# Column blocks of 384, 352 and 352 tokens in place of 368, 368 and 352 in two projections of a streaming encoder layer

## The chip, the cores and the metric

The kernel runs on one core of one Trainium2 chip. The metric is the device time of one execution in microseconds (us), from runs of the whole kernel; the profile comes from one further execution, the profiled one, whose own time is given beside its span.

## What is computed

One layer of a hybrid encoder runs over 1024 prompt frames with 16 meta tokens ahead of them, and over 64 frames of a running stream. All is fp32.

```python
hn = rmsnorm(h, norm_mix_w)
proj = hn @ w_in                      # 1024 -> 3584: xt, b, c, q, k, v, g
conv_out = b * conv3(c * xt)          # causal, depthwise, 512 channels
o = retention(rotary(q), rotary(k), v)   # 4 heads of 128, per-head decay
ret_out = silu(g) * groupnorm(o) * ret_gn_w
h = h + concat([conv_out, ret_out]) @ w_out
f = square(relu(rmsnorm(h, norm_ffn_w) @ w_up)) @ w_down   # 1024 -> 4096 -> 1024
y = rmsnorm(h + f, norm_final_w)
```

The outputs are y for both streams, the last two conv inputs and the retention states.

## The kernel before

Every large product is made of fp32r matmuls on a value split in two parts, hi and lo: `passes` (L1510) issues three matmuls, hi by hi (L1512), hi by lo (L1513) and lo by hi (L1514), and each of them has a weight load of its own, 128x128, before it. In the two projections that the change is about, the activations stand transposed in SBUF, with the 1024 model channels as eight k-tiles of 128 partitions and the tokens as columns; a 128x128 piece of the weight matrix is the stationary operand, and up to 512 token columns stream past it into a PSUM bank.

The work runs in this order:

- Start: the input is normalised, transposed tile by tile into `hn_hi` and `hn_lo`, and `v` is computed.
- In-projection, `iteration` (L1651), four times, one per head and group of 128 channels: six units k, q, g, xt, c, b. A unit is 128 output channels for all tokens. It is done in two halves of four k-tiles (the weight buffers `ws_hi`, `ws_lo` hold one half each), and each half goes over three column blocks of tokens. The lists `CGX` (k, 1104 tokens with the meta tokens), `CGQ` (q, g, b, 1088 tokens) and `CGC` (xt, c, 1090 tokens) give each block's first column and width. A block in a half is 4 k-tiles by 3 passes, so 12 matmuls. A block has a PSUM bank of its own, and the units take two sets of three banks in turn (`set_of`). `bank_free` (L1580) is the wait for the bank. Between blocks the table `AFTER` puts the steps of the retention, `step`, on TensorE.
- Out-projection over nine token tiles, with the second norm and the transposes into `mid_hi` and `mid_lo`.
- FFN, 16 groups of 256 hidden channels. `up` (L1734) computes two units of 128 hidden channels, again in halves of four k-tiles over three column blocks, given by `CGY`. ScalarE takes each block with `relu` (L815) and squares it. Then `product` makes 28 products of 128x128 by 128x512 (the down projection, with seven products in place of eight for each 2x2 block) and `sample` four more for the 64 frames of the running stream. VectorE, ScalarE and GpSimd add them to `h`. The 28 products and the sample are 92 matmuls of 512 columns. The last group ends in plain products and the final norm.

Who takes the blocks of the in-projection: VectorE turns k and q in `rotary` (L1058, four operations for a block, with `rot` of `BLK` columns as scratch) and multiplies c and b; ScalarE takes g and xt. The order of the work on each engine is written out by hand, and no planner decides anything.

Where the column blocks begin and end in SBUF follows from these lines (`TX` is 1104, `TY` 1088, `TP` 1152; the tensors' first bytes are multiples of 128):

```python
        hn_hi = sb("hn_hi", [P, KT, TX], r1, F32R)
        hn_lo = sb("hn_lo", [P, KT, TX], r1 + KT * TX * 4, F32R)
        mid_hi = sb("mid_hi", [P, KT, TP], r2, F32R)
        mid_lo = sb("mid_lo", [P, KT, TY], r2 + KT * TP * 4, F32R)
        rot = sb("rot", [P, BLK], region(BLK * 4))
```

Of the kernel before, what the change touches and what calls it, by code (L numbers as in the profile page):

```python
# [51 lines left out]
TP = TY + SAMPLE  # L52
TILES = (TY + P - 1) // P
XTILES = (TX + P - 1) // P
BLK = 368
CGX = [(0, 368), (368, 368), (736, 368)]
CGQ = [(0, 368), (368, 368), (736, 352)]
CGC = [(0, 368), (368, 368), (736, 354)]
META_AT = [META - 2, META - 1, *range(META - 2)]
CGY = [(0, 368), (368, 368), (736, 352)]  # L60

CONV = [(0, SEQ, META - 2), (SEQ, SAMPLE, META + SEQ)]

UNITS = [("k", 3 * DC + DC, CGX), ("q", 3 * DC, CGQ), ("g", 3 * DC + 3 * DC, CGQ),
         ("xt", 0, CGC), ("c", 2 * DC, CGC), ("b", DC, CGQ)]
V_OFF = 3 * DC + 2 * DC
# [68 lines left out]
def build(nc, x_prompt, x_sample, state_conv, state_ret, meta_tokens, norm_mix_w, w_in, conv_w, ret_gn_w,  # L135
# [3 lines left out]
    with ctx:  # L139
# [4 lines left out]
        def region(size):  # L144
            at = place["at"]
            place["at"] = at + (size + 31) // 32 * 32
            return at

        def sb(name, shape, at, dt=F32):
            return nc.alloc_sbuf_tensor_at(name, shape, dt, offset=at)  # L150
# [71 lines left out]
        onC = sb("onC", [P, HD], region(512))  # L222
        rot = sb("rot", [P, BLK], region(BLK * 4))
        hc = sb("hc", [P, NCONST], region(NCONST * 4))
# [368 lines left out]
        def _(act):  # L593
# [127 lines left out]
            def conv_hi(i, j):  # L721
                act.wait_ge(proj_dve, NX + i * 12 + 9 + j + 1)
                col, n = CGQ[j]
                act.activation(mid_hi[:, bass.ds(i, 1), col:col + n].rearrange("p a c -> p (a c)"),
# [90 lines left out]
            def relu(g, a, j):  # L815
                col, w = CGY[j]
                act.wait_ge(up_done, 6 * g + 3 * a + UP_ORDER[a].index(j) + 1)
                act.activation(fr[:, a, col:col + w], ps[a * 3 + j][:, 0:w], ACT.Relu).then_inc(relu_done, 1)

            def square(g, a, j):  # L820
                col, w = CGY[j]
                act.wait_ge(relu_done, 6 * g + 3 * a + UP_ORDER[a].index(j) + 1)
                act.activation(fr[:, a, col:col + w], fr[:, a, col:col + w], ACT.Square).then_inc(fr_ready, 1)
# [685 lines left out]
        def _(pe):  # L1509
# [224 lines left out]
            def up(g, first):  # L1734
                for a in range(2):
# [5 lines left out]
                    for half, j in order:  # L1741
                        col, w = CGY[j]
                        if j == UP_ORDER[a][0]:
# [127 lines left out]
```

## Time and profile before

| | |
|---|---|
| median of 3 runs | 1223.23 us (1223.08 to 1223.62) |
| the profiled execution | 1223.71 us |
| its span, first to last instruction | 1221.6 us |
| TensorE matmuls, busy | 1211.0 us, 99%, 6669 of them |
| VectorE busy | 757.5 us, 62% |
| ScalarE busy | 523.2 us, 43% |
| GpSimd busy | 300.6 us, 25% |
| the chain of work that ended last | 98% TensorE |
| ScalarE's wait for TensorE before the split of the up weights (L792) | 142.9 us in 29 waits |

The duration of a matmul in the trace is its latency: matmuls overlap, so what one costs in a stream is the distance from its start to the next one's start. The timeline gives starts to 0.01 us, and a block of 12 matmuls is long enough to read that distance to about 1 ns. PE is the matmul, PEld its weight load, DVE is VectorE, ACT ScalarE, POOL GpSimd. The granted clock of TensorE is given as a share of 2.4 GHz.

### The profile page before, as it was taken

To read this page: it belongs to the slowest core of one execution; us is meant where nothing else is said; L and a number is where in the kernel's file an instruction comes from. 1 tells how busy PE (TensorE), PEld (TensorE's weight loads), DVE (VectorE), ACT (ScalarE), POOL (GpSimd) and SP (SyncE) were. 2 spreads that over 40 slices of the span, in tenths; PEclk is the share of its full clock that TensorE was granted. 3 is DMA by queue.
4 is the path that set the end of the run, shared out by engine and by line. 5 is a ranking of instruction groups with operands and counts; after the bars stand their busy time and mean duration, and the time that the engine had idled before them with its cause. 6 is when DMAs were issued, how large, how long until landed. Compare 5 with 4: busy or idle time off the path is not lost.

```text
span 1221.6 us, 20444 instructions
## 1 busy us (share of the span) xinstructions
PE 1211.0 (99%) x6669; PEld 1119.1 (92%) x6669; DVE 757.5 (62%) x1483; ACT 523.2 (43%) x1152; POOL 300.6 (25%) x226
## 2 busy tenths in 40 slices
PE   8999999999999999999999999999999999999997
PEld 6899999999999888989989988998998998998996
DVE  5336665664666363477577568567667667666747
ACT  6424324334343242435434534544444533543546
POOL 0000000000000000253452453453354354345312
PEclk9999999999999999999999999999999999999999
DMA  7011111111112630121022111202201202102104
GB/s 263 25 35 38 39 48 37 47 36 36 47 45 63 173 112 1 52 70 61 17 61 60 39 38 60 63 14 60 69 9 60 69 9 69 60 9 69 52 18 147
DMA packets 85133, 69.58 MB, mean 57 GB/s; under 512 B 9432, under 2 KB 68960, under 8 KB 85104
## 3 DMA queue, kind: packets, MB, share of 16 engines
q1 hardware_dynamic: 84960, 68.95, 18.5%
q8 instruction: 16, 0.26, 0.1%
q10 hardware_dynamic: 144, 0.26, 0.1%
q14 instruction: 13, 0.11, 0.0%
HBM read 64.21 MB, written 4.99 MB: 57 GB/s over the span
## 4 chain that ended last, share of the span: by engine, by line
PE 98%; DVE 1%; ACT 1%; DMA 0%; issue 0%; SPq 0%; DVEq 0%; ACTq 0%
PE pp L1512 30%; PE pp L1514 30%; PE pp L1513 30%; PE pp L1518 1%; PE pp L1519 1%; PE pp L1702 1%; PE pp L1631 1%; PE pp L1642 1%; PE pp L1641 1%; PE pp L1624 1%; PE pp L1529 1%; DMA wv_raw<-in_w_in 0%; PE pp L1613 0%; PE pp L1648 0%; ACT wv_hi L630 0%
## 5 line engine op out<-in xcount | busy, mean ns | idle before, releaser
L1514 PE MATMUL pp<-mid_hi,ws_lo 128*128 128x368 f32 (+1 forms) x768 | 251.3, 327 | 0.0
L1512 PE MATMUL pp<-mid_hi,ws_hi 128*128 128x368 f32 (+1 forms) x768 | 251.2, 327 | 0.0
L1513 PE MATMUL pp<-mid_lo,ws_hi 128*128 128x368 f32 (+1 forms) x768 | 250.7, 326 | 0.0
L1325 DVE TENSOR_TENSOR h<-pp,h 128x512 f32<-128x512 f32 x300 | 194.5, 681 | 6.6 <-PE pp L1514 5.1
L1464 POOL TENSOR_TENSOR h<-tmp,h 128x512 f32<-128x512 f32 x120 | 168.9, 1438 | 115.2 <-ACT tmp L838 115.2
L1512 PE MATMUL pp<-hn_hi,ws_hi 128*128 128x368 f32 (+2 forms) x576 | 192.0, 333 | 0.0
L1514 PE MATMUL pp<-hn_hi,ws_lo 128*128 128x368 f32 (+2 forms) x576 | 189.0, 328 | 0.0
L1513 PE MATMUL pp<-hn_lo,ws_hi 128*128 128x368 f32 (+2 forms) x576 | 189.0, 328 | 0.0
L1512 PE MATMUL pp<-do_hi,fo_hi 128*128 128x512 f32 x452 | 176.3, 390 | 0.2 <-DVE fo_lo L1318 0.2
L1513 PE MATMUL pp<-do_lo,fo_hi 128*128 128x512 f32 x452 | 176.0, 389 | 0.0
L1514 PE MATMUL pp<-do_hi,fo_lo 128*128 128x512 f32 x452 | 175.9, 389 | 0.0
L1281 DVE TENSOR_TENSOR ws_lo<-raw,ws_hi 128x512 fp32r<-128x512 f32 x64 | 59.7, 934 | 140.0 <-ACT ws_hi L792 140.0
L1512 PEld LDWEIGHTS pp<-mid_hi,ws_hi 128*128 128x128 f32 x768 | 144.1, 188 | 0.9 <-DVE mid_lo L1272 0.3
L1513 PEld LDWEIGHTS pp<-mid_lo,ws_hi 128*128 128x128 f32 x768 | 144.2, 188 | 0.6
L1472 POOL TENSOR_TENSOR do_raw<-dr 128x512 f32<-128x512 f32 x15 | 19.3, 1284 | 508.7 <-DMA dr<-in_w_down 508.1
L1514 PEld LDWEIGHTS pp<-mid_hi,ws_lo 128*128 128x128 f32 x768 | 144.2, 188 | 0.0
L838 ACT ACTIVATE tmp<-pp 128x512 f32<-128x512 f32 x120 | 67.5, 598 | 150.5 <-PE pp L1514 150.5
L1512 PEld LDWEIGHTS pp<-hn_hi,ws_hi 128*128 128x128 f32 x576 | 108.4, 188 | 0.1
L1513 PEld LDWEIGHTS pp<-hn_lo,ws_hi 128*128 128x128 f32 x576 | 108.3, 188 | 0.0
L1514 PEld LDWEIGHTS pp<-hn_hi,ws_lo 128*128 128x128 f32 x576 | 108.2, 188 | 0.0
L792 ACT ACTIVATE ws_hi<-raw 128x512 fp32r<-128x512 f32 x64 | 40.1, 628 | 146.1 <-PE pp L1514 142.9
L1512 PEld LDWEIGHTS pp<-do_hi,fo_hi 128*128 128x128 f32 x452 | 84.8, 188 | 18.9 <-DVE fo_lo L1318 0.9
(200 smaller groups left out, 1888.9 us busy)
## 6 DMA issues: line engine op xcount, KB each, us to landing
raw<-in_w_up SPq DMA_DIRECT2D x64, 256.0 KB, 5.1
dr<-in_w_down SPq DMA_DIRECT2D x64, 256.0 KB, 3.5
raw<-in_w_in SPq DMA_DIRECT2D x48, 256.0 KB, 2.9
xr<-in_x_prompt SPq DMA_DIRECT2D x8, 512.0 KB, 6.3
raw<-in_w_out SPq DMA_DIRECT2D x16, 256.0 KB, 3.2
out<-hw SPq DMA_DIRECT2D x9, 256.0 KB, 2.2
wv_raw<-in_w_in SPq DMA_DIRECT2D x8, 256.0 KB, 6.0
h<-in_x_prompt SPq DMA_DIRECT2D x2, 1024.0 KB, 11.3
```

The costliest lines, as they stand in the source:

```text
L792: act.activation(ws_hi[:, half], raw[:, s, :].rearrange("p (k c) -> p k c", k=4), ACT.Copy).then_inc(w_hi, 1)
L838: act.activation(tmp(k), bank_of(p, q)[:, :], ACT.Copy).then_inc(act_copy, 1)
L1281: dve.tensor_tensor(ws_lo[:, half], raw[:, s, :].rearrange("p (k c) -> p k c", k=4), ws_hi[:, half].bitcast(F32), ALU.subtract).then_inc(w ...
L1325: dve.tensor_tensor(h_part(p, q), bank_of(p, q)[:, :], h_part(p, q), ALU.add).then_inc(dve_add, 1)
L1464: pool.tensor_tensor(h_part(p, q), tmp(k), h_part(p, q), ALU.add).then_inc(pool_add, 1)
L1472: pool.tensor_tensor(t1, b12, b11, ALU.subtract).then_inc(d_sum, 1)
L1512: pe.matmul(out, a_hi, b_hi, start=start, stop=False, skip_group_check=again)
L1513: pe.matmul(out, a_hi, b_lo, start=False, stop=False, skip_group_check=again)
L1514: return pe.matmul(out, a_lo, b_hi, start=False, stop=stop, skip_group_check=again)
L1518: pe.matmul(out, a_hi_lo, b_hi, start=start, stop=False)
L1519: return pe.matmul(out, a_hi_lo, b_lo, start=False, stop=stop)
L1529: last = pe.transpose(ps[T1(t)[k // 4]][:, k % 4 * n:k % 4 * n + n], xr[0:n, t % 4, k * P:(k + 1) * P], ident[0:n, 0:n])
```

## The change

In every list of column blocks the border between the first and the second block moves from column 368 to column 384. The first block gets 16 columns more, the second 16 fewer; the third begins at column 736 as before. The scratch `rot` grows by 16 columns, to the widest block.

```diff
-BLK = 368
-CGX = [(0, 368), (368, 368), (736, 368)]
-CGQ = [(0, 368), (368, 368), (736, 352)]
-CGC = [(0, 368), (368, 368), (736, 354)]
+BLK = 384
+CGX = [(0, 384), (384, 352), (736, 368)]
+CGQ = [(0, 384), (384, 352), (736, 352)]
+CGC = [(0, 384), (384, 352), (736, 354)]
 META_AT = [META - 2, META - 1, *range(META - 2)]
-CGY = [(0, 368), (368, 368), (736, 352)]
+CGY = [(0, 384), (384, 352), (736, 352)]
```

No instruction is added, taken away or put elsewhere on any engine: TensorE's program has 1944 rows in both kernels, in the same order, with other widths. On ScalarE, in the first group of the FFN, where `relu` (L818) and the square (L823) take the blocks of the first unit:

```order
 L792 ACTIVATE ws_hi<-raw 128x512
-L818 ACTIVATE fr<-pp 128x368
-L823 ACTIVATE fr<-fr 128x368
-L818 ACTIVATE fr<-pp 128x368
-L818 ACTIVATE fr<-pp 128x352
+L818 ACTIVATE fr<-pp 128x384
+L823 ACTIVATE fr<-fr 128x384
+L818 ACTIVATE fr<-pp 128x352 x2
 L792 ACTIVATE ws_hi<-raw 128x512
```

The same four instructions stand in the same order, the first two 16 columns wider and the next 16 narrower. On VectorE, in the loop of the in-projection, the first piece of the rotary of unit k in the changed kernel:

```order
+L1060 TENSOR_TENSOR kT<-pp,cos_t 128x384
+L1061 REGISTER_ALU
+L1062 TENSOR_TENSOR rot<-pp,sin_t 64x384
+L1063 TENSOR_TENSOR rot<-pp,sin_t 64x384
+L1004 ISA
+L1064 TENSOR_TENSOR kT<-kT,rot 128x384
```

These rows had 368 columns. Nothing else about them is new.

## Rows read from the trace of the kernel before

**Rows 1.** The page: busy time by engine, and the granted clock in 40 slices.

```profile
PE 1211.0 (99%) x6669; PEld 1119.1 (92%) x6669; DVE 757.5 (62%) x1483; ACT 523.2 (43%) x1152; POOL 300.6 (25%) x226
...
PEclk9999999999999999999999999999999999999999
```

**Rows 2.** Waits of PE over the whole span: total us, times, longest us.

```profile
PE pp L1536 <- DVE on L1032: 2.1, 1, 2.1
PE pp L1512 <- DVE hn_lo L1045: 1.6, 1, 1.6
PE pp L1512 <- DVE fo_lo L1318: 0.2, 1, 0.2
```

**Rows 3.** Stretches: length, then busy us of PE, PEld, DVE, ACT, POOL; clock.

```profile
70.00:395.00 325.00, 325.00 (x2082) 324.70 (x2081) 198.74 (x606) 116.26 (x296) 0.00 (x0) 1.00 0.15 42
540.00:1192.00 652.00, 652.00 (x3466) 600.31 (x3465) 429.73 (x661) 297.56 (x616) 275.59 (x200) 1.00 0.15 46
```

**Rows 4.** Timeline of PE, one FFN group, first matmul of each block: start, duration.

```profile
676.66 0.33 PE L1512 MATMUL pp<-mid_hi,ws_hi 128*128 128x368 f32 x1
...
678.66 0.33 PE L1512 MATMUL pp<-mid_hi,ws_hi 128*128 128x368 f32 x1
...
680.68 0.32 PE L1512 MATMUL pp<-mid_hi,ws_hi 128*128 128x352 f32 x1
...
682.58 0.33 PE L1512 MATMUL pp<-mid_hi,ws_hi 128*128 128x368 f32 x1
...
684.59 0.33 PE L1512 MATMUL pp<-mid_hi,ws_hi 128*128 128x368 f32 x1
...
686.61 0.32 PE L1512 MATMUL pp<-mid_hi,ws_hi 128*128 128x352 f32 x1
...
688.52 0.33 PE L1512 MATMUL pp<-mid_hi,ws_hi 128*128 128x368 f32 x1
...
690.53 0.33 PE L1512 MATMUL pp<-mid_hi,ws_hi 128*128 128x368 f32 x1
...
692.54 0.32 PE L1512 MATMUL pp<-mid_hi,ws_hi 128*128 128x352 f32 x1
...
694.45 0.33 PE L1512 MATMUL pp<-mid_hi,ws_hi 128*128 128x368 f32 x1
...
696.46 0.33 PE L1512 MATMUL pp<-mid_hi,ws_hi 128*128 128x368 f32 x1
...
698.48 0.32 PE L1512 MATMUL pp<-mid_hi,ws_hi 128*128 128x352 f32 x1
...
700.38 0.40 PE L1512 MATMUL pp<-do_hi,fo_hi 128*128 128x512 f32 x1
```

**Rows 5.** Timeline of PE: the first matmul behind that group's 92 of 512 columns.

```profile
721.28 0.33 PE L1512 MATMUL pp<-mid_hi,ws_hi 128*128 128x368 f32 x1
```

**Rows 6.** Timeline of PE, in-projection: seven blocks of 368, then one of 352.

```profile
151.12 0.33 PE L1512 MATMUL pp<-hn_hi,ws_hi 128*128 128x368 f32 x1
...
165.20 0.32 PE L1512 MATMUL pp<-hn_hi,ws_hi 128*128 128x352 f32 x1
...
167.13 0.27 PE L1616 MATMUL pp<-ident,kT 128*128 128x128 f32 x1
```

**Rows 7.** Groups of instructions, shapes apart: busy us, mean ns, idle before.

```profile
L818 ACT ACTIVATE fr<-pp 128x368 f32<-128x368 f32 x64 | 30.3, 474 | 32.9 <-PE pp L1514 32.9
...
L818 ACT ACTIVATE fr<-pp 128x352 f32<-128x352 f32 x32 | 14.9, 465 | 16.1 <-PE pp L1514 16.1
```

**Rows 8.** Timeline, an FFN group: the operand of the ninth product, and that product.

```profile
659.62 1.23 DVE L1318 TENSOR_TENSOR fo_lo<-fr,fo_hi 128x512 fp32r<-128x512 f32 x1
...
661.23 0.40 PE L1512 MATMUL pp<-do_hi,fo_hi 128*128 128x512 f32 x1
```

**Rows 9.** Timeline, in-projection: end of the rotary of q, and its reader.

```profile
178.98 0.53 DVE L1064 TENSOR_TENSOR qT<-qT,rot 128x352 f32<-128x352 f32 x1
...
180.93 0.33 PE L1627 MATMUL pp<-qT,kT 128*128 128x64 f32 x2
```

## The prediction

> **What bounds the kernel now.** I read the page first: PE is busy 99% of the span, and no other engine over 62%; the granted clock stands at its upper level, 2.4 GHz, in every slice [rows 1]. Then PE's waits: three in the whole span, together 3.9 us, and only 0.2 us of that after the start [rows 2]. Then the two stretches in which the change works: in the middle of the in-projection PE is busy 325.00 of 325.00 us, in the FFN 652.00 of 652.00, both at clock 1.00 [rows 3]. So the reader is to see that nothing feeds PE too late, and that the time is the sum of the distances between matmul starts. The change keeps the number of matmuls and the number of columns. It can only matter if a matmul's distance isn't a straight line in its width, or if a shifted block border makes PE wait. The timeline tells the first.
>
> **Distances before.** One FFN group has twelve blocks of 12 matmuls between 676.66 and 700.38 us [rows 4]. The four blocks of 352 take 1.90, 1.91, 1.91 and 1.90 us, so 7.62 / 48 = 158.75 ns a matmul. The four pairs of 368 take 4.02, 4.03, 4.02 and 4.03, so 16.10 / 96 = 167.7 ns. The 92 matmuls of 512 columns run from 700.38 to 721.28 [rows 4, 5], so 20.90 / 92 = 227.2 ns. At 2.4 GHz the columns alone are 146.7, 153.3 and 213.3 ns; what is over is 12.1 ns at 352, 14.4 at 368 and 13.9 at 512. The 352 block is cheaper than a line through the other two would have it: 16 columns between 352 and 368 cost 9.0 ns where the clock asks for 6.7. That is the whole room that the change has in the FFN.
>
> In the in-projection this is not so. Seven blocks of 368 run from 151.12 to 165.20, so 14.08 / 84 = 167.6 ns, and the next one of 352 takes 1.93 us, 160.8 ns [rows 6]. The step is 6.8 ns, almost what 16 columns take at the clock.
>
> One thing in the code goes with this difference, and I take it as a working idea that no row proves. In the FFN the block at column 736 begins and ends at multiples of 128 bytes in all k-tiles (736 x 4 is 23 x 128, and the k-tiles lie 36 or 34 x 128 bytes apart). Column 368 is 11.5 x 128. In the in-projection the k-tiles are 34.5 x 128 bytes apart, so half of all rows are off such a border whatever the columns are. If whole pieces are cheap and broken ones dear, the new border, column 384 (12 x 128), helps in the FFN and hardly at all in the in-projection.
>
> **The change, part by part.**
>
> *FFN, 64 halves of a unit (16 groups, two units, two halves).* A half has now a block of 384 and one of 352 in place of two of 368. The second 352 block begins on a border like the third, and I give it the third's 158.75 ns. No row has 384 columns. The nearest rows bound it so. Low: the 352 block and 32 columns at the clock, 158.75 + 13.3 = 172.1 ns. On the line from 352 to 512 it is 158.75 + 0.2 x 68.4 = 172.4. On the line from 368 to 512 it is 167.7 + 59.5 / 9 = 174.3. High: the dear step of 9.0 ns once more, 176.7. I take 172.5, since 352 and 512 are the two widths whose blocks lie wholly on the borders, as the new one does. A pair of blocks is then 12 x (172.5 + 158.75) = 3.975 us against 4.025, and 64 pairs give 3.2 us. The ends: 172.1 gives 12 x 4.55 ns x 64 = 3.5 us, 174.3 gives 12 x 2.35 x 64 = 1.8 us, 176.7 gives nothing.
>
> *In-projection, 48 halves (four heads, six units, two halves).* By its own rows 352 is 160.8 ns and 384 on the same line is 167.6 + 6.7 = 174.3; the pair is 335.1 against 335.2, so 12 x 0.1 x 48 = 0.06 us, nothing. The ends: if 384 costs 172.5 there too, 12 x 1.9 x 48 = 1.1 us is gained; if it costs 176.6, 1.2 us is lost.
>
> *The takers of the blocks.* ScalarE's relu is 474 ns at 368 and 465 at 352 [rows 7]; the first block grows by some 9 ns and the second shrinks by as much. That lies beside PE's blocks of 1.9 us and costs nothing. If it did not, the first to be late would be the ninth product of a group: its operand's low part begins at 659.62 and has ended by 659.62 + 1.23 = 660.85, and the product starts at 661.23, with 0.38 us to spare [rows 8]. What leads to it (relu of the last block, its square, two sums, the split) begins with the end of the third block, which keeps its width and its distance to the products, so the 0.38 us stay. In the in-projection the tightest that I looked at is the rotary of q, ended at 178.98 + 0.53 = 179.51 for a matmul at 180.93, 1.4 us to spare [rows 9]. The first block's four operations get wider and the second's narrower, and the last one ends as before.
>
> *PSUM banks and weights.* Each block keeps its own bank, and 384 columns fit in one of 512. The second block starts 12 x 4.8 = 58 ns later than before and the third 50 ns earlier than before (in the FFN), far less than the slack above. Weight loads are the same in number and size; PEld has 92% of the span busy beside PE [rows 1] and no wait of its own in these stretches.
>
> *Sum.* 3.2 us less, on the profiled execution's 1223.71 us: 1220.5. The median of the runs is 0.5 us under the profiled one, so by it 1223.23 - 3.2 = **1220.0 us**.
>
> **The rivals.** A measurement of this kernel can tell about 0.2% from no change, that is 2.45 us.
>
> 1. *A straight line.* A matmul costs its columns at the clock and a fixed part that belongs to its place in the half, not to its width. For it speaks the in-projection, where the two widths differ by the clock's share [rows 6]; against it that the FFN's step is 9.0 ns [rows 4], but the cheap block there is always the third, so place and width can't be told apart. Then the second block of 352 costs what the second of 368 did less 6.7 ns, the first 6.7 more: gain nothing, **1223.2 us**. The Trainium skill's page TensorE: Matmul & The Clock Gate, section Back-to-back issue gap, gives the start-to-start distance as columns over the clock with 2.5 ns on top. By that rule any split of 1088 columns in three costs the same, and the sum is 1223.2; on the fixed part the trace differs, with 12 to 14 ns, and on the line it agrees in the in-projection and not in the FFN.
>
> 2. *Half of it.* 352 is cheap at column 384 as well, but 384 lies on the line of 368 and 512, at 174.3 ns: 1.8 us less, **1221.4 us**.
>
> 3. *Both stages gain.* 384 costs 172.5 in the in-projection too: 3.2 + 1.1, **1218.9 us**. Against it speaks that the off-border rows are there at any column.
>
> 4. *Slower.* The dear step goes on with width: 384 costs 9.0 ns more than 368 (176.7 in the FFN, 176.6 in the in-projection), and the middle block doesn't get the third's price, but 167.7 - 6.7 = 161.0 ns. In the FFN a pair is then 337.7 against 335.4, so 12 x 2.3 x 64 = 1.8 us more; in the in-projection 337.4 against 335.2, 12 x 2.2 x 48 = 1.3 us more: **1226.3 us**. It decides as soon as 384 costs over 174.4 ns with a middle block of 161. For it is only the one step between 352 and 368; against it is 512, whose 13.9 ns over the clock are less than those of 368.
>
> **How the numbers follow.** The forecast has 0.45, half of it 0.20, a straight line 0.20, both stages 0.08, slower 0.07. Faster by over 0.2% means under 1220.8: the forecast and both stages, 0.53. Slower by over 0.2% means over 1225.7: 0.07. The rest, half of it and the straight line, 0.40. The range reaches from 1218.8, the case of both stages at its price, to 1223.8, the straight line with the half microsecond by which the three runs differ among themselves. Left out are the slower case and the edges of the others, about 0.15. The likeliest case alone would be 1219.6 to 1220.8.
>
> **What would show it right or wrong.** In the timeline of the changed kernel an FFN group's twelve blocks should take 12 x (172.5 + 158.75 + 158.75) x 4 = 23.52 us in place of 23.72, with 2.07 us for a block of 384 and 1.90 for either of 352. If the second block takes 1.94 us and the first 2.09, the straight line is right. In the in-projection 384 should take 2.09 us and 352 1.93. PE's waits should be the same three. A fourth, or a longer one before a product or a block, would make the forecast wrong in a way that I gave no price. So would a 384 block over 2.12 us.

## The result, and the profile after

The change made the kernel slower: 1225.29 us (median of 19 runs, 1224.38 to 1226.13) against 1223.53 (19 runs, 1222.64 to 1224.00), a ratio of 1.0015 with a 95% interval of 1.0008 to 1.0021. The forecast was 1220.0 us, with a range from 1218.8 to 1223.8. The profiled execution took 1224.96 us, with a span of 1222.9, where before it was 1223.71 and 1221.6.

The page of the changed kernel, busy time and granted clock, against [rows 1]:

```profile
PE 1212.2 (99%) x6669; PEld 1120.6 (92%) x6669; DVE 757.4 (62%) x1483; ACT 522.6 (43%) x1152; POOL 300.7 (25%) x226
...
PEclk9999999999999999999999999999999999999999
```

PE has 1.2 us more and PEld, its weight loads, 1.5; no other engine has more than 0.1 more. The waits of PE in the changed kernel (total us, times, longest us), against [rows 2]:

```profile
PE pp L1536 <- DVE on L1032: 2.1, 1, 2.1
PE pp L1512 <- DVE hn_lo L1045: 1.5, 1, 1.5
PE pp L1529 <- DVE xr L1038: 0.3, 1, 0.3
```

They all lie in the start; the block borders brought no wait. The stretches of [rows 3] in the changed kernel:

```profile
70.00:395.00 325.00, 325.00 (x2080) 324.73 (x2079) 198.66 (x606) 116.25 (x296) 0.00 (x0) 1.00 0.15 42
540.00:1192.00 652.00, 652.00 (x3460) 600.60 (x3459) 429.00 (x660) 296.14 (x614) 275.73 (x200) 1.00 0.15 46
```

The stretches are as full and the clock as high as before, but fewer matmuls fit in them: 2080 for 2082, and 3460 for 3466. So the distances between starts have grown. The timeline of PE in the changed kernel, first half of a unit and the beginning of the next half in the same FFN group as [rows 4]:

```profile
677.02 0.33 PE L1512 MATMUL pp<-mid_hi,ws_hi 128*128 128x384 f32 x1
...
679.13 0.32 PE L1512 MATMUL pp<-mid_hi,ws_hi 128*128 128x352 f32 x1
...
681.05 0.32 PE L1512 MATMUL pp<-mid_hi,ws_hi 128*128 128x352 f32 x1
...
682.97 0.34 PE L1512 MATMUL pp<-mid_hi,ws_hi 128*128 128x384 f32 x1
```

The block of 384 takes 2.11 us (2.07 was forecast), the second block 1.92 to 1.93 (1.90) and the third 1.91 to 1.92 (1.90). Inside the first block of a second half, matmul by matmul:

```profile
682.97 0.34 PE L1512 MATMUL pp<-mid_hi,ws_hi 128*128 128x384 f32 x1
683.14 0.34 PE L1513 MATMUL pp<-mid_lo,ws_hi 128*128 128x384 f32 x1
683.32 0.35 PE L1514 MATMUL pp<-mid_hi,ws_lo 128*128 128x384 f32 x1
683.50 0.34 PE L1512 MATMUL pp<-mid_hi,ws_hi 128*128 128x384 f32 x1
683.68 0.34 PE L1513 MATMUL pp<-mid_lo,ws_hi 128*128 128x384 f32 x1
683.86 0.33 PE L1514 MATMUL pp<-mid_hi,ws_lo 128*128 128x384 f32 x1
684.03 0.33 PE L1512 MATMUL pp<-mid_hi,ws_hi 128*128 128x384 f32 x1
```

The first five distances are 175, 177, 185, 176 and 182 ns; from then on each is 173.3. Those five cost 28 ns more than the steady ones. The timeline prints 0.01 us; the starts in the trace are whole nanoseconds, and what stands in ns from here on is read from them. A whole group's twelve blocks take 23,784 ns in every one of the 15 groups that have them together, to 1 ns; before it was 23,723. So the difference is not chance. That the traffic of other engines doesn't make it is likely from this, but not shown, since their work repeats with the groups too.

By stages, from the first matmul of a stage to its last: the in-projection took 327.55 us before and 327.87 after, the FFN with all that follows 717.97 and 719.11. So 0.3 us were lost in the one and 1.1 in the other. Of the 1.1, 16 groups times 61 ns make 1.0, and the 92 matmuls of 512 columns in each of the other groups, 227.16 ns on average for 226.92, make 0.3; in the first group they gave 0.15 back, most of it at the late operand of [rows 2], where the distance before the ninth product fell from 565 to 468 ns.

### The profile page after: what moved, and what is told of

It is laid out like the page before. It is cut to its first block, busy times and chain, and to the rows that moved or that the text cites. A ratio compares the mean times of both kernels' runs of the same rounds, so it can differ in the third digit from the quotient of the medians.

```text
span 1222.9 us, 20444 instructions
## 1 busy us (share of the span) xinstructions
PE 1212.2 (99%) x6669; PEld 1120.6 (92%) x6669; DVE 757.4 (62%) x1483; ACT 522.6 (43%) x1152; POOL 300.7 (25%) x226
## 4 chain that ended last, share of the span: by engine, by line
PE 96%; DMA 1%; DVE 1%; issue 1%; ACT 1%; SPq 0%; POOL 0%; DVEq 0%; POOLq 0%; ACTq 0%
PE pp L1512 30%; PE pp L1513 30%; PE pp L1514 30%; PE pp L1518 1%; PE pp L1519 1%; PE pp L1702 1%; PE pp L1631 1%; PE pp L1642 1%; PE pp L1641 1%; PE pp L1624 1%; PE pp L1529 1%; DMA xr<-in_x_prompt 1%; DMA dr<-in_w_down 0%; PE pp L1648 0%; PE pp L1613 0%
## 5 line engine op out<-in xcount | busy, mean ns | idle before, releaser
L1512 PE MATMUL pp<-mid_hi,ws_hi 128*128 128x352 f32 (+1 forms) x768 | 251.2, 327 | 0.1
L1514 PE MATMUL pp<-mid_hi,ws_lo 128*128 128x352 f32 (+1 forms) x768 | 251.3, 327 | 0.0
L1513 PE MATMUL pp<-mid_lo,ws_hi 128*128 128x352 f32 (+1 forms) x768 | 250.9, 327 | 0.0
L1512 PE MATMUL pp<-hn_hi,ws_hi 128*128 128x352 f32 (+3 forms) x576 | 191.9, 333 | 0.0
L1513 PE MATMUL pp<-hn_lo,ws_hi 128*128 128x352 f32 (+3 forms) x576 | 189.3, 329 | 0.0
L1514 PE MATMUL pp<-hn_hi,ws_lo 128*128 128x352 f32 (+3 forms) x576 | 188.8, 328 | 0.0
L1512 PE MATMUL pp<-do_hi,fo_hi 128*128 128x512 f32 x452 | 176.2, 390 | 0.1
L1513 PE MATMUL pp<-do_lo,fo_hi 128*128 128x512 f32 x452 | 176.0, 389 | 0.0
L1513 PEld LDWEIGHTS pp<-mid_lo,ws_hi 128*128 128x128 f32 x768 | 144.6, 188 | 0.6
L1512 PEld LDWEIGHTS pp<-mid_hi,ws_hi 128*128 128x128 f32 x768 | 144.2, 188 | 1.0 <-DVE mid_lo L1272 0.4
L1513 PEld LDWEIGHTS pp<-hn_lo,ws_hi 128*128 128x128 f32 x576 | 108.3, 188 | 0.0
L1512 PEld LDWEIGHTS pp<-hn_hi,ws_hi 128*128 128x128 f32 x576 | 108.3, 188 | 0.1
L1512 PEld LDWEIGHTS pp<-do_hi,fo_hi 128*128 128x128 f32 x452 | 84.8, 188 | 18.6 <-DVE fo_lo L1318 0.8
```

The costliest lines, as they stand in the source:

```text
L1512: pe.matmul(out, a_hi, b_hi, start=start, stop=False, skip_group_check=again)
L1513: pe.matmul(out, a_hi, b_lo, start=False, stop=False, skip_group_check=again)
L1514: return pe.matmul(out, a_lo, b_hi, start=False, stop=stop, skip_group_check=again)
```

## The experiments

All blocks below are of the up projection, in ns for 12 matmuls, first, second and third block of a half, in the 15 groups behind the first; they repeat there to 1 ns, in a few kernels to 3. Where a label's kernel was run once, its total is one run and tells little; the blocks are read from its trace.

**Each stage alone.** e1_ffn_only has only `CGY` changed, e2_in_only only the other three lists and `BLK`.

> Only the up projection has blocks of 384, 352 and 352; the in-projection keeps 368, 368 and 352 or more. From the traces: an FFN group's twelve blocks take 23.78 us in place of 23.72, and if all of the loss of the change lies there, the time is 1.0 to 1.8 us over that of before (1224.6 to 1225.3 beside 1223.5). If the loss came from the in-projection or from elsewhere, it is within 0.3 us of before.

> Only the in-projection has the border at 384; the up projection is as before. If the FFN makes the loss, this is 0.2 to 0.4 us over before, which is what the changed kernel's trace is late at the end of the in-projection. If the in-projection makes it, 1.0 us or more.

Measured: 1224.32 us against 1223.54, ratio 1.0010 (1.0001 to 1.0019), and 1223.75, ratio 1.0003 (0.9994 to 1.0012). The FFN group took 23,784 ns in the first and 23,723 in the second; the in-projection 327.55 and 327.86 us. So each stage loses by itself, and the FFN's loss is the larger. By its total e2 can't be told from before. e1's total is a little under its expected 1.0; in its trace the first group of products has no late operand and gains 0.5 us against that of before.

**Place.** e3_place changes the order of widths in the up projection, a list for each unit:

```diff
-CGY = [(0, 368), (368, 368), (736, 352)]
+CGY = [[(0, 352), (352, 384), (736, 352)],
+       [(0, 352), (352, 352), (704, 384)]]
```

> Up projection only: the first unit of a group has blocks of 352, 384, 352, the second 352, 352, 384. Theory of history (a matmul of 384 costs 173.3 ns in the steady state and the first five behind a narrower block cost 28 ns more together): a block of 384 takes 2.11 us wherever it stands, since it always follows one of 352. Theory of place (the fixed part belongs to the place in the half): 384 takes 2.10 us in the middle and 2.06 us as the third, and 352 takes 1.93 us as the first and in the middle, 1.90 us as the third.

Measured: 384 took 2106 to 2110 ns in the middle and 2108 to 2109 as the third, so place is not the point. History as I had put it isn't either: in the middle block the dear matmuls (182, 176) come back every five and don't settle. And one result fits neither. The third block of 352 of the first unit took 1899 ns in the first half and 2001 in the second, each in all 15 groups. The timeline of that second half, first matmul of each block:

```profile
682.76 0.32 PE L1513 MATMUL pp<-mid_hi,ws_hi 128*128 128x352 f32 x1
...
684.68 0.34 PE L1513 MATMUL pp<-mid_hi,ws_hi 128*128 128x384 f32 x1
...
686.79 0.33 PE L1513 MATMUL pp<-mid_hi,ws_hi 128*128 128x352 f32 x1
...
688.79 0.32 PE L1513 MATMUL pp<-mid_hi,ws_hi 128*128 128x352 f32 x1
```

The last block, 2.00 us for 352 columns, has 166 or 167 ns in each of its distances, 8 to 9 ns more than the same block in the half before. (L1513 stands for L1512 where a kernel has a line more.) The same width can settle in more than one rhythm.

**Where the stream is read.** e4_read leaves the widths of before, e7_read384 those of the changed kernel, and both let TensorE read from other columns (`at` in place of `col` in the operand only):

```diff
+READ = [[0, 352, 736], [0, 368, 720]]      # e4; e7: [[0, 368, 736], [16, 384, 736]]
...
-                                          mid_hi[:, kk, col:col + w], mid_lo[:, kk, col:col + w],
+                                          mid_hi[:, kk, at:at + w], mid_lo[:, kk, at:at + w],
```

> Widths as before, but in the up projection TensorE reads some blocks from other columns, so that the output of these tokens is that of others (part of the computation is changed): in the first unit the second block of 368 reads from column 352, which is a multiple of 128 bytes, and in the second unit the third block of 352 reads from column 720, which is not. Theory of borders: the second block falls from 2.02 us to 2.00 us in the first unit, and the third rises from 1.90 us to 1.93 us in the second. Theories of place and of history: 2.02 and 1.90 as before.

> The changed kernel's widths; in the up projection TensorE reads some blocks from other columns, so that the output of these tokens is that of others (part of the computation is changed). First unit: the second block, 352 wide, reads from column 368, off a border of 128 bytes. Second unit: the first block, 384 wide, reads from column 16, off one. Theory of borders: 1.93 us rises to 1.95 or more, and 2.11 rises to 2.13 or more. If only the width counts: 1.93 and 2.11 as in the changed kernel.

Measured in e4: the second block fell from 2018 to 2000 and the third rose from 1902 to 1922, both as borders of 128 bytes would have it. Measured in e7: the opposite. The 384 columns read from column 16, off a border, took 2082 in place of 2108; in the first unit the second block, off a border, fell from 1927 to 1916. But the third behind it, which was read from where it was, rose from 1911 to 1998, the rhythm of 167 ns again, and the block of 384 behind that one, read from column 0, took 2080. So the address of the stream counts, and a border alone doesn't say how. e4 by itself would have confirmed a wrong idea. (The tokens of the blocks that are read elsewhere come out wrong in these kernels; the work of TensorE is the same.)

**Borders in the in-projection.** e8_stride sets the rows of `hn_hi` and `hn_lo` 1120 columns apart, so that all k-tiles lie whole multiples of 128 bytes apart. It also moves all that lies behind them, the stream of the up projection and the weight buffers too, by 1024 bytes.

> The kernel before, with the rows of the normalised input 1120 in place of 1104 columns apart, so that all k-tiles of the in-projection begin at multiples of 128 bytes; nothing else changes. Theory of borders: the in-projection's blocks of 352 fall from 1.93 to 1.90 us as in the FFN, 40 of them (354 too, less), and some of the 368 by 0.01 to 0.02: 1 to 1.5 us less, 1222.0 to 1222.5. If borders don't matter: the same as before within 0.3 us.

Measured: 1223.44 us against 1223.26, ratio 1.0001 (0.9992 to 1.0010), and the stage 327.47 us for 327.55. In the first half of unit g the blocks went from 2009, 2014, 1935 to 2037, 1998, 1913: two cheaper by 16 and 22 ns, the first dearer by 28. The forecast's idea failed here too. The FFN, whose stream and weights had both moved by 1024 bytes, kept its blocks to 1 ns and its 23,723 for the group. One thing about borders was never sure: the kernel rounds the address at which its tensors begin to 32 bytes, and no line shows it to be a multiple of 128.

**Other widths.** e5_even has 364, 364, 360 in one unit and 368, 360, 360 in the other; e6_wide 400, 336, 352 and 384, 384, 320.

> Up projection only, nearly even blocks: 364, 364, 360 in the first unit of a group, 368, 360, 360 in the second. Theory of the floor (a matmul costs its columns and 32 cycles of 2.4 GHz, as the steady 384 and 512 do): 165.0 ns for 364 and 163.3 for 360, so 5.92 us for a half, as before (5.93). If broken pieces of 128 bytes cost, most blocks here begin or end off a border and are dearer: 167 ns for 364 and 166 for 360, 5.99 us for a half.

> Up projection only, all blocks on borders of 128 bytes or 64: 400, 336, 352 in the first unit, 384, 384, 320 in the second. Theory of the floor: 180.0 ns for 400, 173.3 for 384, 153.3 for 336, 146.7 for 320. If 384 is dear as a width, both blocks of 384 take 2.11 us (175.7 ns) again, else 2.08. If the narrow blocks are held by something that doesn't depend on columns, 336 and 320 stay at 158 ns as 352 does; otherwise they fall by 6.7 ns for 16 columns.

Measured: e5's halves took 5.95 to 5.99 us, against 5.92 to 5.94 before, with blocks of 360 that settle at 167 ns and one that alternates between 159 and 168. The columns plus 32 cycles, 5.92, failed here; that 5.99 was the other idea's number supports it little, since e7 and e8 speak against that idea. In e6 the columns plus 32 cycles held within a nanosecond for most: 180.3 ns for 400, 153.1 for 336, 146.0 for 320, 173.3 for the second 384. The first 384 took 2082 in one half and 2108 in the other. 400, 336 and 352 took 5.913 to 5.917 us in both halves of their unit, the cheapest unit so far of a kernel with all its columns in place; before has 5.918 to 5.938.

**Code, weights, or both.** e9_weights64 puts 64 bytes ahead of the two weight buffers of the changed kernel, which moves them and all that lies behind them; e10_code adds an instruction between the first group and the loop over the others; e11_shift reads from columns 16 and 400, and 32 and 416.

```diff
+        region(64)
         ws_hi = sb("ws_hi", [P, 2, 4, P], region(4096), F32R)
```

```diff
+            pe.sem_inc(code_shift, 1)
             with pe.Fori(1, G_LAST) as g:
```

> The changed kernel with the two weight buffers (and all that lies behind them) 64 bytes further on in SBUF; the columns are read from where they were. If the extra nanoseconds come from where the weight load and the stream read at the same time, the block times of an FFN group move: the 28 ns of the first block of 384 go or come elsewhere, and 1.93 and 1.91 us change by 10 ns or more. If only the widths, or only the streamed columns' addresses, set them: 2108, 1927 and 1911 ns again, to 1 ns.

> The changed kernel with one more instruction on TensorE ahead of the loop over the FFN groups, a semaphore increment that nobody waits for, so that the loop's code lies elsewhere. If the block times come from how the instructions are fetched, they change in the loop; if not, 2108, 1927 and 1911 ns again, to 1 ns.

> The changed kernel's widths; in the up projection TensorE reads the first and second block 16 columns further on in the first unit (columns 16 and 400) and 32 columns further on in the second (32 and 416), so that the output of these tokens is that of others (part of the computation is changed). Reading from column 16 took the first block from 2108 to 2080 ns. If it is the half piece of 128 bytes that does it, column 32 gives 2108 again and column 16 gives 2080 and 1916. If it is the address at some larger scale, column 32 gives something else. If only the width counts, both are 2108 and 1927.

Measured: e10 gave 2106 to 2109, 1927 to 1928, 1911, in every half of the loop as in the changed kernel, 23,784 ns for the group. Where the loop's code lies does nothing. The first group, which lies ahead of the new instruction and is the same in both kernels, holds a surprise. The last block of its first unit and the first matmul behind it, in the changed kernel and in e10:

```profile
507.96 0.32 PE L1512 MATMUL pp<-mid_hi,ws_hi 128*128 128x352 f32 x1
...
509.86 0.34 PE L1512 MATMUL pp<-mid_hi,ws_hi 128*128 128x384 f32 x1
```

```profile
507.76 0.33 PE L1513 MATMUL pp<-mid_hi,ws_hi 128*128 128x352 f32 x1
...
509.76 0.33 PE L1513 MATMUL pp<-mid_hi,ws_hi 128*128 128x384 f32 x1
```

The same code at the same addresses took 1900 ns in the one and 2000 in the other, the rhythms of 158 and 167 ns. PE had stood still ahead of the block before it, for 77 ns in the one and 81 in the other; but e1 has 81 too and took 1900, so which difference in time decides is not shown. What is shown is that widths and addresses don't fix a rhythm alone.

e9 changed all blocks though not one streamed address moved: 2098 and 2127 in the first unit and 2077 in the second for 384, 1919 to 1937, 1917 to 1922. In e11 column 16 gave 2081, 1919, 1903 and column 32 gave 2106 and 2110, as column 0 does, but then 2001 and 2000 for 352 in the second half. So both addresses count, the weight load's and the stream's. With the first two blocks read from column 16 the changed kernel's halves took 5.900 to 5.904 us, less than any half of before (5.918): with other addresses the changed widths might have won.

**Their distance.** e12_both64 moves the stream's buffer and the weights by 64 bytes. e15_w64_before does to the kernel before what e9 did to the changed one. e13_mid64 and e14_mid64_before were meant to move the stream's buffer alone by 64 bytes, in the changed kernel and in that of before. But their edit does more: the region is 128 bytes longer, so the weight buffers and all behind them lie 128 bytes further on. The distance from the stream to the weights grows by 64 bytes in e13 and e14, just as in e9 and e15.

```diff
-        r2 = region(KT * (TP + TY) * 4)
+        r2 = region(KT * (TP + TY) * 4 + 128) + 64      # e13, e14
```

> The changed kernel with both the streamed input of the up projection and the weight buffers 64 bytes further on, so that their distance is as in the changed kernel. Theory of the meeting (what counts is the streamed address relative to the weight load's): the FFN's blocks take 2108, 1927 and 1911 ns again. Theory of borders (each access counts by its own place against a border of 128 bytes): they differ by 10 ns or more, since both are now off a border.

> The changed kernel with the input of the up projection alone 64 bytes further on, a correct kernel. Theory of the meeting: the first block falls to 2080 ns, as it did when it was read from column 16, and the second to 1916 to 1920; the third is open, 1900 to 1998. With 1903 for it a half takes 5.90 us in place of 5.95, 64 x 0.05 = 3 us less than the changed kernel, 1222. If the third locks at 167 ns a matmul, a half takes 6.0 us, 3 us more than the changed kernel. If the address doesn't count: 1225.3.

> The kernel before with the input of the up projection alone 64 bytes further on. Its first block now begins off a border of 128 bytes, its second on one, its third off. Theory of the meeting: the block times change, with the second from 2020 to about 2000 ns, as when it was read from column 352; a half stays between 5.90 and 6.0 us. If the address doesn't count: 1998 to 2013, 2019 and 1903 ns again, 1223.5 us.

> The kernel before with the weight buffers alone 64 bytes further on. Theory of the meeting: a shift of the weights by 64 bytes does to the blocks what a shift of the stream by 64 bytes the other way does, and since 64 is half of 128 the FFN's block times are those of the kernel with the streamed input shifted, to a few ns. Theory of borders: they differ from these as well as from those of before. The in-projection's blocks change too in either case.

| kernel | stream, weights moved by | unit 1, half 2 | unit 2, half 1 | group |
|---|---|---|---|---|
| changed | 0, 0 | 2108, 1928, 1911 | 2108, 1927, 1911 | 23,784 |
| e12 | 64, 64 | 2108, 1928, 1911 | 2108, 1928, 1911 | 23,763 |
| e9 | 0, 64 | 2127, 1937, 1922 | 2077, 1920, 1917 | 23,753 |
| e13 | 64, 128 | 2127, 1937, 1922 | 2077, 1920, 1917 | 23,753 |
| before | 0, 0 | 2013, 2020, 1905 | 2008, 2018, 1902 | 23,723 |
| e15 | 0, 64 | 2032, 1987, 1921 | 2032, 1987, 1921 | 23,750 |
| e14 | 64, 128 | 2032, 1987, 1921 | 2032, 1987, 1921 | 23,769 |

With both moved by the same 64 bytes, the changed kernel's rhythm comes back, but for the first block of the group (2082 for 2106) and the last (1914 for 1911). e9 and e13, with a distance 64 bytes larger but at different places, have the same blocks to a nanosecond or two, and so have e15 and e14 with the other widths; only in the first half of a group, behind the products, they differ by up to 13 ns, and in its last block by 2 or 3. So in three pairs of kernels (changed and e12, e9 and e13, e15 and e14) an equal distance gave equal blocks though the buffers lay elsewhere, and e8 agrees. The timelines of e9 and of e13, second half of the first unit:

```profile
684.08 0.34 PE L1513 MATMUL pp<-mid_hi,ws_hi 128*128 128x384 f32 x1
...
686.21 0.32 PE L1513 MATMUL pp<-mid_hi,ws_hi 128*128 128x352 f32 x1
...
688.15 0.32 PE L1513 MATMUL pp<-mid_hi,ws_hi 128*128 128x352 f32 x1
...
690.07 0.33 PE L1513 MATMUL pp<-mid_hi,ws_hi 128*128 128x384 f32 x1
```

```profile
684.42 0.34 PE L1512 MATMUL pp<-mid_hi,ws_hi 128*128 128x384 f32 x1
...
686.54 0.32 PE L1512 MATMUL pp<-mid_hi,ws_hi 128*128 128x352 f32 x1
...
688.48 0.32 PE L1512 MATMUL pp<-mid_hi,ws_hi 128*128 128x352 f32 x1
...
690.40 0.33 PE L1512 MATMUL pp<-mid_hi,ws_hi 128*128 128x384 f32 x1
```

Both show 2.12 to 2.13, 1.93 to 1.94 and 1.92 us. What counts, as far as addresses do, is where the stream's stands relative to the weight load's. That it is the two reads that meet while a matmul runs is the likely reading and not shown: other tensors behind the weights moved with them, though TensorE reads none of these in the up projection. Nor does any run show that 64 bytes one way do what 64 bytes the other way do, on which the expectation of e15 rests. The stream alone, nearer to the weights, moved only in e11, for two blocks of three: 2077 to 2081, 1919 and 1903, which are not the blocks of e13. In time, e13 was 1226.07 us (ratio 1.0021, 1.0012 to 1.0031), e14 1226.42 (1.0023, 1.0014 to 1.0033) and e15 1224.55 (1.0009, 0.9999 to 1.0018), all against 1223.41. My 2080 for the first block of e13 came in one unit (2077) and not in the other (2104 and 2127), and the third block brought none of the 3 us that I held possible. Both numbers came from a stream moved against weights that stood still, which e13 isn't. What it did gain was 31 ns a group, and in the in-projection, with the weights 128 bytes further on, 0.6 us (327.27 for 327.87); something else took 2.3 us, told of below. e12's one run took 1227.68 us, which has the same 2.3 in it and another 1.4 in the in-projection.

**A better order, and 128 bytes.** e16_400 is the kernel before with 400, 336 and 352 in the up projection; e17_400_w128 has the weight buffers 128 bytes further on as well.

```diff
-CGY = [(0, 368), (368, 368), (736, 352)]
+CGY = [(0, 400), (400, 336), (736, 352)]
```

> The kernel before with blocks of 400, 336 and 352 in both units of the up projection. These took 2166, 1837 and 1914 ns (2162 in the second half) in one unit of an earlier run, 5.915 us for a half, against 5.918 to 5.938 before. Theory of the meeting: the order of widths sets where stream and load meet, and both units now repeat this; 64 halves are 1.0 us less in the FFN than before, 1222.5 beside 1223.4. If each unit settles in another pattern, as blocks of the same widths did elsewhere, 1223 to 1225.

> The same with the weight buffers 128 bytes further on. If only the distance within 128 bytes counts, the FFN's blocks are those of the kernel with 400, 336 and 352 to a few ns. In the in-projection a shift of the buffers by 128 bytes went with 0.3 to 0.6 us less (327.3 us for the stage), which would come back here: 1222.2.

Measured: e16 took 1222.23 us against 1223.41, ratio 0.9990 (0.9981 to 0.9999), as expected from its blocks: 2162, 1837 and 1914 ns in nearly every half, 23,657 ns for a group, and an FFN of 717.05 us for 717.97. It beats the kernel before by 0.1%, and the changed one's 1225.29 of another session by about 0.25%. e17 took 1227.10 us, ratio 1.0029 (1.0018 to 1.0039). The timelines of e16 and e17, the same half:

```profile
682.61 0.34 PE L1512 MATMUL pp<-mid_hi,ws_hi 128*128 128x400 f32 x1
...
684.77 0.31 PE L1512 MATMUL pp<-mid_hi,ws_hi 128*128 128x336 f32 x1
...
686.61 0.33 PE L1512 MATMUL pp<-mid_hi,ws_hi 128*128 128x352 f32 x1
...
688.52 0.35 PE L1512 MATMUL pp<-mid_hi,ws_hi 128*128 128x400 f32 x1
```

```profile
683.47 0.34 PE L1513 MATMUL pp<-mid_hi,ws_hi 128*128 128x400 f32 x1
...
685.67 0.32 PE L1513 MATMUL pp<-mid_hi,ws_hi 128*128 128x336 f32 x1
...
687.54 0.33 PE L1513 MATMUL pp<-mid_hi,ws_hi 128*128 128x352 f32 x1
...
689.46 0.34 PE L1513 MATMUL pp<-mid_hi,ws_hi 128*128 128x400 f32 x1
```

128 bytes turn 2.16, 1.84, 1.91 into 2.20, 1.87, 1.92, and 4.9 us are lost in the FFN. So shifts of the distance by whole 128 bytes count too; what period it has is open. In the in-projection e17 took 327.16 us for 327.57, the expected 0.3 to 0.6 less.

## Why the prediction was wrong

**What held.** PE is the bound, and the time is the sum of the distances between starts: no wait came behind the start, the clock stayed, and the takers of the blocks cost nothing, as forecast. That the change can only matter by the price of a width was right too.

**The step that failed** is the price of the blocks in the FFN: the 172.5 ns for 384, and the second 352 block, "I give it the third's". The steady distance at 384 is 173.3 ns, near the forecast. But a block of 384 took 2108 ns, 175.7 a matmul, where 2070 were forecast, and 64 of them make 2.4 us. The second block took 1928 for 1905, 1.5 us. The third, which I left as it was, took 1911 for 1904, 0.5 us. Together 4.4 us, which turn the forecast gain of 3.2 into a loss of 1.2; the groups show 1.0. The high end of my bounds for 384, 176.7 ns, held its 175.7, but I had tied it to a step that goes on with width, and gave it 0.07.

**Why it failed.** I took the average of a block as a property of its width. The cheap 352 block of before, 12 ns over the clock, has the same width as the block that costs 14 ns over it in the second place of the changed kernel, and the same columns as the one that costs 20 in e3. The working idea of borders of 128 bytes explained the two numbers that I had, and no third was there to test it; e7 and e8 refuted it. What a block costs depends, at one width, on the distance between the stream's and the weights' addresses (e9, e13, e14, e15) and on what ran before it (e3, e10). Why the addresses of the changed kernel give just these prices stays open. The bounds for 352 should have been the two prices in the trace of before, 158.75 and 160.8 ns, and not one of them.

**In-projection.** Forecast was nothing, measured 0.32 us lost. The price of the undisturbed blocks was nearly right: 2.095 to 2.102 us for 384, where 2.09 was forecast, and 1.93 for 352. The few nanoseconds by which most blocks of 384 were over, and the third block of unit k, which rose from 2.01 to 2.02 us, make up the loss; some blocks went the other way.

**The rivals.** The slower one gave 1226.3 for the measured 1225.3. Its prices, 176.7 and 161.0 ns, are near the 175.7 and 160.6 of the FFN; its reason, a dear step that goes on with width, is wrong, since 400 costs 180.3 (e6). In the in-projection its price for 384 was too high. The straight line held roughly, for the steady distances of 320, 384, 400 and 512 columns at about 32 cycles over the columns, but not for the blocks of 352 and 368. It also had the better reading of the trace of before: that the cheap 352 belongs to something else than its width. That something was not the place but the addresses and what ran before.

The first rival takes the columns and 2.5 ns from the Trainium skill for a stream like this one. The section that it names, Back-to-back issue gap of the Trainium skill's page TensorE: Matmul & The Clock Gate, gives that formula for the isolated matmul; in a stream of pairs of load and matmul, it says, both set the spacing, and at 512 columns the formula counts too much. Here it counts too little, 216 ns for the 227 of the traces.

The Trainium skill, page TensorE: Matmul & The Clock Gate, section Step-by-step: what each phase is for, says that the array has two independent read ports in SBUF and that loading the next weights doesn't take read bandwidth from the running matmul. It says nothing of addresses there. Here, with the same instructions, the time of a block moved by 43 ns in 2166 when the weight buffers and what lies behind them were put 128 bytes further on (e16, e17). Whether read bandwidth is what is lost, and so whether the sentence fails here, no run shows.

## What to carry to other kernels

In a stream where each matmul has a weight load of its own, a width has no price by itself. In these runs the averages of blocks of 320 to 400 columns lay between 2 ns under and 7 ns over the columns and 32 cycles at 2.4 GHz, depending on the addresses and on what ran before; let no forecast rest on a difference of 3 ns between two block averages. When such a kernel is tuned to 0.1%, moving by 64 or 128 bytes a buffer that TensorE reads is a change like any other (up to 4.9 us here); before believing in a new tiling, time it with its buffers in two or three places. And test an explanation where it says something new: e4 agreed with the borders, e7, its mirror image, did not. Then work out where every buffer lies after an edit: e13 and e14 moved two things and not one.

## What was not expected of the hardware

- A group's time repeats to 1 or 2 ns over 15 groups, and the distances follow short cycles: 155, 159, 158, 162 ns for 352 columns before, a steady 160 or a steady 167 elsewhere.
- A shift of 64 bytes of the tensor that holds the stationary operand of the out-projection (e12, e13, e14) cost 2.3 us between the in-projection and the FFN, 104.14 to 104.20 us for 101.86, over 416 matmuls of 512 columns, 5.5 ns each. With the weight buffers alone moved, by 64 (e9) or 128 bytes (e17), it stayed 101.79 and 101.88. Those 2.3 us are why e13 and e14 are slower than their FFN stages say. The weight buffers 64 bytes further on cost the in-projection of the changed kernel 1.4 us (e9, 329.23 for 327.87, and e12, 329.25), that of the kernel before 0.4 (e15, 327.94 for 327.55); 128 bytes further on gave 0.3 to 0.6 back.
- Why the distance of the two addresses costs what it does, which of its bits decide it, and how a rhythm of 167 ns keeps itself up, stays open.
